# A hybrid attention and gated-MLP block on eight cores: the gating unit moved behind the attention, a part of the gate logits put in its place

## What is computed

```python
h = rmsnorm(x, norm1_g)                       # x: (4, 4096, 1024) float32
q, k, v, f_logit, u, sv, gates = split(h @ w_in)   # 512, 512, 512, 8, 512, 512, 2048 columns
logf = log_sigmoid(f_logit + b_f)
y_a = forgetting_attention(q, k, v, logf) @ w_a    # 8 heads of 64, causal, cumulated log gates added
v2 = layernorm(gelu(sv), ln_v_g, ln_v_b)           # per 128 positions: mixed by w_sgu, per group of 64
y_b = (gelu(u) * (mix(v2, w_sgu) + b_sgu)) @ w_b
g_a, g_b = split(gates)
x = x + (sigmoid(g_a) * y_a + sigmoid(g_b) * y_b) @ w_o
x = x + square(relu(rmsnorm(x, norm2_g) @ w_up)) @ w_down
return rmsnorm(x, normf_g)
```

## Time and profile before

| | us |
|---|---|
| median of 3 runs | 1326.27 |
| lowest and highest | 1326.08, 1328.8 |
| the profiled execution | 1336.07 |
| span of its slowest core (core 7) | 1334.5 |
| span of its fastest core (core 0) | 1314.7 |

### The profile page before, as it was taken

One profiled execution on the slowest core, in us unless ns is written; L12 is line 12 of the kernel. 1 busy time (PEld: TensorE's weight loads), 2 busy tenths in 40 slices (PEclk: granted clock), 3 DMA queues, 4 the chain that ended last, 5 costly groups with the idle time before them and its releaser, 6 DMA issues.

```text
span 1334.5 us, 22415 instructions; the slowest of 8 cores (1314.7 to 1334.5 us)
## 1 busy us (share of the span) xinstructions
PE 1172.6 (88%) x7624; PEld 577.1 (43%) x7624; DVE 585.0 (44%) x951; ACT 482.1 (36%) x634; POOL 305.0 (23%) x278
## 2 busy tenths in 40 slices
PE   4577887869899878887999997999999999999994
PEld 1234444435455444444444443444444444444441
DVE  2355473243224666664222233653433434334357
ACT  2212224547788655665222223421111121111153
POOL 0112130110001434331322220033333232332320
PEclk9787978989999878997999998999999999999998
DMA  7824033151122113101431216332130320303015
GB/s 141 206 77 151 29 121 93 49 105 40 45 53 49 27 34 63 26 21 41 71 64 25 48 16 166 106 53 45 19 64 1 64 52 13 64 0 64 1 64 189
DMA packets 30942, 85.42 MB, mean 64 GB/s; under 512 B 5088, under 2 KB 13376, under 8 KB 25248
## 3 DMA queue, kind: packets, MB, share of 16 engines
q0 software_dynamic: 5312, 31.18, 14.2%
q1 hardware_dynamic: 25232, 52.78, 13.4%
q10 hardware_dynamic: 288, 0.03, 0.0%
HBM read 99.88 MB, written 13.17 MB: 85 GB/s over the span
## 4 chain that ended last, share of the span: by engine, by line
PE 75%; DVE 8%; DMA 8%; issue 4%; ACT 3%; SPq 1%; DVEq 0%; POOL 0%; ACTq 0%; POOLq 0%
PE pss L362 75%; ACT PT L366 2%; DMA xres<-xown 1%; DVE VP L384 1%; DMA QpT<-QT 1%; DMA WK<-wproj 1%; DVE hown L380 1%; DVE zz L380 1%; DMA scrt<-kst 1%; DMA xbuf<-xown 1%; DMA WQ<-wproj 1%; DVE hprev L380 1%; DMA xbuf<-xprev 1%; DVE uT L380 1%; DMA QpT<-scrq 1%
## 5 line engine op out<-in xcount | busy, mean ns | idle before, releaser
L366 ACT ACTIVATE PT<-pss 128x1024 bf16<-128x1024 f32 (+1 forms) x288 | 271.3, 973 | 161.7 <-PE pss L362 160.8
L374 DVE TENSOR_TENSOR x1T<-pss,x1T 128x512 f32<-128x512 f32 x256 | 176.1, 691 | 247.6 <-PE pss L362 219.2
L362 PE MATMUL pss<-QpT,KpT 86*128 86x512 bf16 (+3 forms) x640 | 179.2, 368 | 59.4 <-ACT PT L366 41.5
L362 PE MATMUL pss<-aT,fdn 128*128 128x512 bf16 x1024 | 226.7, 379 | 0.6 <-DVE x1T L374 0.6
L362 PE MATMUL pss<-h2T,fup 128*128 128x512 bf16 x1024 | 226.2, 379 | 0.0
L366 ACT ACTIVATE rl<-pss 128x512 f32<-128x512 f32 x128 | 76.3, 597 | 333.3 <-PE pss L362 327.8
L374 POOL TENSOR_TENSOR aT<-rl 128x512 bf16<-128x512 f32 x128 | 133.5, 1044 | 264.4 <-ACT rl L366 248.9
L362 PEld LDWEIGHTS pss<-aT,fdn 128*128 128x128 bf16 x1024 | 100.1, 98 | 121.7 <-issue 1.4
L362 PEld LDWEIGHTS pss<-h2T,fup 128*128 128x128 bf16 x1024 | 100.2, 98 | 120.8
L362 PEld LDWEIGHTS pss<-VP,PT 128*128 128x128 bf16 x2176 | 106.5, 101 | 78.9 <-issue 37.3
L362 PE MATMUL pss<-VP,PT 128*128 128x65 bf16 x2176 | 119.6, 199 | 16.4 <-DVE VP L384 15.9
(11 more groups left out here) (117 smaller groups left out, 1064.1 us busy)
## 6 DMA issues: line engine op xcount, KB each, us to landing
xbuf<-xown SPq DMA_DIRECT2D x8, 1024.0 KB, 8.3
xbuf<-xprev SPq DMA_DIRECT2D x8, 1024.0 KB, 9.1
xres<-xown SPq DMA_DIRECT2D x32, 256.0 KB, 3.2
fup<-w_up POOLq DMA_DIRECT2D x8, 1024.0 KB, 9.5
fdn<-w_down POOLq DMA_DIRECT2D x8, 1024.0 KB, 10.8
out<-ostg SPq DMA_DIRECT2D x32, 256.0 KB, 2.1
Wb<-wmrg POOLq DMA_DIRECT2D x8, 768.0 KB, 8.4
scrt<-kst SPq DMA_DIRECT2D x32, 128.0 KB, 2.8
```

The lines of the kernel that those rows point to most:

```text
L362: S.op("pe", lambda e, a=(out, lhsT, rhs, start, stop): e.matmul(a[0], a[1], a[2], start=a[3], stop=a[4]), r, w)
L366: S.op("act", lambda e, a=(out, in_, func, scale): e.activation(out=a[0], in_=a[1], func=a[2], scale=a[3]), r, w)
L374: S.op(eng, lambda e, a=(out, in0, in1, op): e.tensor_tensor(a[0], a[1], a[2], a[3]), r, w)
```

## The change

- **The gating unit leaves chunk 3.** It runs behind the last head as a stage of its own, with all 8 PSUM banks as its ring. Its gelu is now one ACT function (`AF.Gelu`) that reads the PSUM bank; the hand-made chain with `xs`, `zz` and `gg` goes. The last product (`vln`) moves from POOL to DVE.
- **Gate logits go into chunk 3.** For the first three of eight column blocks (NLG = 3) the 24 pairs of dc, I and branch are computed as fill pieces (`lg_q`), copied by DVE to float tiles `lg`, and used in merging in place of 16 of the 24 matmuls of these 12 rounds. Their weights `Wg` lie where `hprev` was. WU and WSV are loaded behind the first column block's logits, not as soon as the x buffers are free.
- **Squares** are taken on ACT alone, in eight pieces of 512 columns, woven between other pieces; before, POOL took 10 of the 16 halves of 2048 columns.
- **x loads** are in quarters, and from position 1 on they are issued on the POOL queue, not on SP. Position 1 is issued before WK. The start computes V of both positions first, then K and Q.
- **`wsTb`** is loaded at the end of chunk 0, and the DVE memset on it stands there too.
- **Banks**: a head's sums always lie in bank 4; the fill ring has banks 5, 6 and 7; the transposes of `yst` take a ring bank.
- Ln and Exp behind `rms_q` and `f_q` are written one or two pieces later (`later`).

```diff
+        WU, WSV = [at(n, 4096, BF16, OFF_W + 8 * KB * i) for i, n in enumerate(("WU", "WSV"))]
+        lg = [at("lg%d" % i, 512, F32, OFF_X0 + 2 * KB * i if i < 20 else OFF_W + (16 + 2 * (i - 20)) * KB) for i in range(24)]
+        Wg = [at("Wg%d" % i, 16 * 128, BF16, OFF_HP + 4 * KB * i) for i in range(2)]
+        g32 = [at("g32%d" % i, 512, F32, OFF_VP + (16 + 2 * i) * KB) for i in range(4)]
+        vln = [at("vln%d" % i, 512, BF16, OFF_VP + (24 + i) * KB) for i in range(4)]
+        stmp = [at("stmp%d" % i, 512, F32, OFF_VP + (28 + 2 * i) * KB) for i in range(2)]
+        uT = at("uT", 4 * T, BF16, OFF_VP, False)
...
+        Wb = [at("Wb%d" % i, 24 * 128, BF16, OFF_HP + 6 * KB * i) for i in range(2)]
...
-        def xload(pos, r=()):
+        def xload(pos, eng="pool"):
             own, I = order[pos]
             src = xown_d if own else xprev_d
             i_ = pos % 2
-            for hf in range(2):
-                ld("sp", xbuf[i_][:, hf * 2048:(hf + 1) * 2048], src[I, :, hf * 2048:(hf + 1) * 2048], B("xb%d%d" % (i_, hf)), r)
+            for hf in range(4):
+                bf = B("xb%d%d" % (i_, hf))
+                S.dma(eng, lambda e, a=(xbuf[i_][:, hf * 1024:(hf + 1) * 1024], src[I, :, hf * 1024:(hf + 1) * 1024]): e.dma_start(out=a[0], in_=a[1]),
+                      [], [bf], bf if eng == "pool" else Buf("xs%d" % hf))
...
-        xload(0)
+        xload(0, "sp")
         ld("pool", onesb[:], cst_d[:, 256:384], B("onesb"))
         ld("pool", wf[:], wf_d[:, :], B("wf"))
-        ld("pool", WV[:], wproj_d[0], B("WV"), [B("xb01")])
+        ld("pool", WV[:], wproj_d[0], B("WV"), [B("xb03")])
+        xload(1)
         ld("pool", WK[:], wproj_d[1], B("WK"))
-        xload(1, [B("WK")])
-        ld("pool", WQ[:], wproj_d[2], B("WQ"), [B("xb11")])
-        ld("sp", trif[:], cst_d[:, 128:256], B("trif"))
+        ld("pool", WQ[:], wproj_d[2], B("WQ"))
+        ld("sp", bexp[0:32, :], bexp_d[:, 0:32], B("bexp"))
+        ld("sp", trif[:], cst_d[:, 128:256], B("trif"), [B("xb13")])
...
+        def sq_q(pos):
             i_ = pos % 2
-            for hf, eng in enumerate(engs):
-                src, dst = xbuf[i_][:, hf * 2048:(hf + 1) * 2048], sq[:, hf * 2048:(hf + 1) * 2048]
-                if eng == "act":
-                    act(dst, src, AF.Square, [B("xb%d%d" % (i_, hf))], [B("sq%d" % hf)])
-                else:
-                    tt(eng, dst, src, src, ALU.mult, [B("xb%d%d" % (i_, hf))], [B("sq%d" % hf)])
+
+            def mk(kc):
+                return (0.0, lambda: act(sq[:, kc * 512:(kc + 1) * 512], xbuf[i_][:, kc * 512:(kc + 1) * 512], AF.Square,
+                                         [B("xb%d%d" % (i_, kc // 2))], [B("sq%d" % kc)]))
+            return [mk(kc) for kc in range(8)]
...
+        def lg_q(dc, I, j):
+            li = (dc * 4 + I) * 2 + j
+            wg = Wg[dc % 2]
+
+            def mms(pb, kc):
+                mm(ps(pb), wg[:, j * 1024 + kc * 128:j * 1024 + (kc + 1) * 128], hown[:, kc * T + I * 512:kc * T + (I + 1) * 512], kc == 0, kc == 7,
+                   [B("Wg%d" % (dc % 2)), B("ho%d_%d" % (kc, I))], [PB[pb]])
+
+            def evict(pb):
+                cp("dve", lg[li][:], ps(pb), [PB[pb]], [B("lg%d" % li)])
+            return unit_q(mms, evict)
+
+        def gload(dc):
+            ld("pool", Wg[dc % 2][:], wmrg_d[dc][:, 1024:3072], B("Wg%d" % (dc % 2)))
...
+                gt, gB = g32[b % 4], B("g32%d" % (b % 4))
+                s6, s6B, b4 = st6[b % 2], B("st6%d" % (b % 2)), b % 4
+                act(gt[:], ps(pb), AF.Gelu, [PB[pb]], [gB])
+                S.op("dve", lambda e, a=(s6[:, 0:6], gt[:]): e.bn_stats(a[0], a[1]), [gB], [s6B])
+                S.op("dve", lambda e, a=(mv[b4][:, 0:2], s6[:, 0:6]): e.bn_aggr(a[0], a[1]), [s6B], [B("mv%d" % b4)])
+                ts("dve", tv[b4][:], mv[b4][:, 1:2], EPS, None, ALU.add, ALU.bypass, [B("mv%d" % b4)], [B("tv%d" % b4)])
+                tt("pool", rsv[b4][:], tv[b4][:], mhalf[:], ALU.pow, [B("tv%d" % b4), B("mhalf")], [B("rsv%d" % b4)])
 
                 def nrm():
-                    gt, gB, b4 = gg[b % 2], B("gg%d" % (b % 2)), b % 4
                     ts("dve", gt[:], gt[:], mv[b4][:, 0:1], rsv[b4][:, 0:1], ALU.subtract, ALU.mult, [gB, B("mv%d" % b4), B("rsv%d" % b4)], [gB])
-                    tt("pool", vln[b % 6][:], gt[:], lng[:], ALU.mult, [gB, B("lng")], [B("vln%d" % (b % 6))])
+                    tt("dve", vln[b4][:], gt[:], lng[:], ALU.mult, [gB, B("lng")], [B("vln%d" % b4)])
                     vdone.add(b)
-                late.append([4, fin])
-                late.append([6, nrm])
+                later(2, nrm)
...
+                act(uT[:, cc * T + I * 512:cc * T + (I + 1) * 512], ps(pb), AF.Gelu, [PB[pb]], [B("uT%d_%d" % (I, q_)) for q_ in range(4)])
...
+            ld("pool", wsTb[:], wsT_d[:, :], B("wsTb"))
+            memset("dve", wsTb[64:128, :].rearrange("p (g i) -> p g i", i=128)[:, :, 0:64], 0.0, [B("wsTb")], [B("wsTb")])
...
-        squares(0, ("act", "act"))
-        run(rms_q(0))
+        run(sq_q(0) + rms_q(0))
+        flush_late()
         run(stt_q(0))
-        xload(2, [B("WQ")])
-        run(f_q(0))
-        for blk in range(4):
-            run(v_q(0, blk))
-        squares(1, ("act", "act"))
-        for p in range(4):
-            run(kq_q(0, p, False))
+        xload(2)
+        run(v_q(0, 0) + v_q(0, 1) + sq_q(1) + v_q(0, 2) + v_q(0, 3) + f_q(0))
         run(rms_q(1))
+        flush_late()
         run(stt_q(1))
         xload(3)
-        run(f_q(1))
-        run(kq_q(1, 0, False))
-        run(fin_tot(0))
-        run(kq_q(1, 1, False))
-        run(fin_cum(0))
-        run(kq_q(1, 2, False))
-        for kind in range(3):
-            run(fin_tr(0, kind))
-        run(kq_q(1, 3, False))
-        run(v_q(1, 0))
+        run(v_q(1, 0) + f_q(1) + v_q(1, 1) + v_q(1, 2) + fin_tot(0) + v_q(1, 3))
+        run(kq_q(0, 0, False) + fin_cum(0) + kq_q(1, 0, False) + kq_q(0, 1, False) + fin_tr(0, 0) + kq_q(0, 2, False) + fin_tr(0, 1) + fin_tr(0, 2))
         run(kq_q(0, 0, True))
         headload(0)
-        squares(2, ("act", "pool"))
-        for blk in range(1, 4):
-            run(v_q(1, blk))
-        for p in range(1, 4):
-            run(kq_q(0, p, True))
+        run(kq_q(0, 3, False) + kq_q(1, 1, False) + kq_q(1, 2, False) + kq_q(1, 3, False))
         headload(1)
-        ring[:] = [6, 7]
-
-        memset("dve", wsTb[64:128, :].rearrange("p (g i) -> p g i", i=128)[:, :, 0:64], 0.0, [B("wsTb")], [B("wsTb")])
+        run(weave(kq_q(0, 1, True) + kq_q(0, 2, True) + kq_q(0, 3, True), sq_q(2), 2))
+        flush_late()
+        ring[:] = [5, 6, 7]
...
+            t1 = kq_q(e, 1, False) + kq_q(o, 1, True) + [("pair", (c, 1))]
             t2 = kq_q(o, 2, False) + kq_q(e, 2, False) + kq_q(o, 2, True)
             if c < 3:
-                qs += rms_q(o + 2) + ev(lambda: squares(e + 2, ("pool", "pool")))
+                qs += weave(t1, sq_q(o + 2), 2)
+                qs += rms_q(o + 2)
...
+        NLG = 3
+
+        def lg_list():
+            qs = []
+            for dc in range(NLG):
+                for I in range(4):
+                    for j in range(2):
+                        qs += lg_q(dc, I, j)
+                if dc + 2 < NLG:
+                    qs += ev(lambda dc=dc: gload(dc + 2))
+                if dc == 0:
+                    qs += ev(lambda: (ld("pool", WU[:], wproj_d[3], B("WU")), ld("pool", WSV[:], wproj_d[4], B("WSV"))))
...
-            yb = 4 + n % 2
+            yb = 4
...
+                        tb = fbank()
                         for qb in range(4):
-                            mm(pss[:, yb * 512 + qb * 128:yb * 512 + (qb + 1) * 128], yst[yi][:, qb * 128:(qb + 1) * 128], identb[:], True, True,
-                               [B("yst%d" % yi), B("identb")], [PB[yb]])
-                        cp("dve", yaT[:, p * T + I * 512:p * T + (I + 1) * 512], ps(yb), [PB[yb]], [B("ya%d_%d" % (p, I))])
+                            mm(pss[:, tb * 512 + qb * 128:tb * 512 + (qb + 1) * 128], yst[yi][:, qb * 128:(qb + 1) * 128], identb[:], True, True,
+                               [B("yst%d" % yi), B("identb")], [PB[tb]])
+                        cp("dve", yaT[:, p * T + I * 512:p * T + (I + 1) * 512], ps(tb), [PB[tb]], [B("ya%d_%d" % (p, I))])
...
-                    wload()
+                    gload(0)
+                    gload(1)
...
+        ring[:] = [0, 1, 2, 3, 5, 6, 7, 4]
+        rk[0] = 0
+        bundle(0)
+        bundle(1)
+        run(ev(bias2))
+        for b in range(16):
+            run(sv_q(b) + u_q(b))
+            if b >= 3 and b % 4 == 3:
+                run(mix_q(b - 3) + (mix_q(b - 2)))
+            elif b >= 4 and b % 4 == 0:
+                run(mix_q(b - 2))
+            elif b >= 4 and b % 4 == 1:
+                run(mix_q(b - 2))
+        run(mix_q(14) + mix_q(15))
...
+                st_ = dc < NLG
+                for kc in range(0 if st_ else 8):
...
+                for j in range(2):
```

(3 more changed lines are left out.)

190 lines of the change are left out of this document (74 added, 116 removed).

## The result

The changed kernel takes **1286.36 us** (median of 4 runs, 1284.68 to 1287.47), the kernel before 1327.53 us (1326.08 to 1329.22): ratio 0.969, interval 0.967 to 0.971. It is 41 us faster, where 62.5 were forecast; 1264 was the time named and 1238 to 1292 the range, so the result lies in its upper part. Times of kernels leave out executions in which one die ran clearly longer at a lower granted clock. The profiled execution took 1284.68 us, on its slowest core (core 0) 1283.2; the fastest core had 1270.4.

What follows compares the result with a forecast made beforehand. Chunk 3's attention was held by ACT's queue waiting for DVE's hand-made gelu. Gains of 27 (chunk 3, gating, merging), 14.5 (start), 7, 11, 2 (chunks 0 to 2) and 1 sum to 62.5 us: 1264 us, range 1238 to 1292.

Steps and rivals of the forecast that it cites:

- Rival (b): Chunk 3 stays ragged, ACT pacing its steps at clock 0.89: stage 165 us, kernel 1288 us; chance 15%.
- the shifts: Chunk 3: third ring bank 5 us off; Wg wait 3, WU and WSV loads 3, single y bank 1 on.
- The third bank: Chunk 3: a third ring bank takes away most short waits for VP copies, 5 us off.
- Rival (a): Gating stage runs at PE's pace, DVE's wait for POOL hidden: 20 us less, kernel 1244 us; chance 12%.
- (c): Gating stage runs at 1.2 GHz because PE pauses for DVE: 40 us more, kernel 1304 us; chance 7%.
- (d): Kernel slower than before, over 82 of 183 us PE work in chunk 3 and gating at 1.2 GHz; chance 3%.
- rival (e): New start and load order bring nothing, memory being at its limit: 1285 us; chance 6%.
- the waits for QpT: Chunk 1: PE's waits of 10.1 and 4.7 us go with the WU and WSV transfers, 14.8 us less.
- The 4 us for VP: Chunk 1: part of the 6.3 us of waits for VP goes, 4 us less.
- The `wsTb` term: Chunk 1: DVE's memset waits for the late wsTb load, holding yst and a K copy: 8 us lost, 4 to 12.
- Banks 3 us less, y bank 1 us more: Chunk 2: third ring bank gains 3 us, single bank for head sums costs 1, net 2 us less.
- so nothing new comes to bound it: Merging: DVE's 1.38 us and POOL's 1.26 us still fit a 1.73 us round; stage 127.5 us.

Runs made afterwards that it cites:

- the version with slots: Changed kernel with merging's first three short weight blocks in own tiles, loaded with block 3 at the gating stage's start, Wo's load late: 1269.65 us, ratio 0.957.

## Why the prediction was right, and where it was off

**Direction and cause: right.** Chunk 3 was ragged because ACT's queue stood behind DVE: the run without Tanh took 51 us off it (at most 17 of them the Tanhs' own time), and the changed chunk has clock 1.00 and 6.3 us of waits for Exps. Rival (b) fell.

**Chunk 3, 141 forecast, 135.6 measured.** The base, chunk 2's ratio of 1.14 times 122, gives 139; the shifts added 2. The Wg wait (3 us) and the contention of WU and WSV with head loads (3 us) didn't occur: no wait for either is in the list. The third bank was counted at 5 us for `VP` waits, which chunk 3 hardly has: no V is made there. The 5 us came off all the same, by another cause than forecast: the ratio came from chunk 2, which carries some 6 us of those waits, and the new chunk 3 has none. So 139 - 5 + 1 = 135 is what remains of the sum, and 135.6 was measured.

**Gating stage, 82 forecast, 75.7 measured.** The mechanism holds (DVE's 16 waits for `rsv`, confirmed by moving the normalisation). The size was high by a term taken from a stage in which POOL was loaded: statistics to the end of the power took 1.99 us (562.69 to 564.68) and not 2.29, with the power at 0.55 and not 0.84 us, and an sv unit without mixings went round in 3.35 us, not 3.9. Rival (a), the stage at PE's pace, is nearly what the edit made of it: 66.8 us, where 61 were counted. Rivals (c) and (d) fell: the granted clock was 0.92 in this stage and not near 0.5. PE did pause, 11.4 us in four places, and the clock is lowest where it did, in the last quarter of the stage:

```profile
540.00:560.00 20.00, 19.82 (x124) 8.97 (x123) 14.47 (x30) 6.24 (x11) 2.19 (x4) 1.00 0.00 1
...
580.00:598.80 18.80, 10.06 (x77) 4.82 (x75) 13.63 (x28) 6.68 (x10) 2.19 (x4) 0.84 0.01 2
```

The Trainium skill's case (TensorE: Matmul & The Clock Gate, "A second HAM failure mode: psum-queue depth-cycling"), by which (c) would have been likeliest, is not borne out by the trace: 0.84 is the lowest of its four quarters. The price of (d) was also added up wrongly: all 183 us at 1.2 GHz would have given 1264 + 183 - 20 = 1427 us, not 1365.

**Start and chunk 0: right**, within 1 us each, and rival (e) fell. In the start the course fits too: V of position 0 ended at 33 us (32 forecast), the scaling of position 1 began at 35. For chunk 0 the number fits, and the scalings are 0.75 us at most, where the earlier trace rows had 5.83 for two; but what those were worth to PE no run isolates, and the chunk's median moves by 2 us by itself.

**Chunk 1, 106 forecast, 106.8 measured: luck.** The forecast was 11 us less; the median fell by 2.1, from 108.9. The sum started from core 7, where the chunk took 117 us and the waits for QpT of the earlier trace rows came to 14.8 us. Core 6 had 14.2 us of them, the six others 7.0 to 9.2 us and a chunk of 108 to 110 us. So some 6 us of this term were a gain on two cores only. The 4 us for VP did not come either: PE still waits 6.1 us there. The `wsTb` term was 8 us (4 to 12), and its removal gave 12.1 us of the median, at the top of its range, as the clock's part was left out; the single bank for the sums, which the sum of this chunk left out, cost 3.0 us more. That these errors end at 106.8 is chance: the base was 8 us too high for the median, and the losses were put too low.

**Chunk 2, 105 forecast, 109.4 measured: wrong sign.** "Banks 3 us less, y bank 1 us more" failed on both halves. The `VP` waits came from a dependency on a name, not from a bank, and so stayed at 6.1 us; the single bank for the sums cost 2.4 us, not 1.

**Merging, 127.5 forecast, 148.5 measured: the step that failed.** It is the sentence "so nothing new comes to bound it", which looked at DVE and POOL only and put the weights' landing at nothing. The count of matmuls was right, as the version with slots shows. Missing was the question that the same text puts elsewhere: what is late next. Three blocks became three times as short, their weights kept one block of cover, and Wo's 2 x 1024 KB still stood between two of them. The earlier trace rows had the price: 11.2 us for 1024 KB, against 6.9 us of cover.

**Output projection, 1 forecast, 6.6 us less measured.** PE's wait at its end, of the kernel before and then of the changed one:

```profile
PE pss L362 <- ACT sq L366: 7.6, 3, 6.2
```
```profile
PE pss L359 <- ACT sq L363: 0.6, 1, 0.6
```

On the seven other cores of the kernel before this wait was 3.2 to 5.4 us, so its going is the larger part of the 6.6 us, not all of it. That more `xres` buffers are the reason was not tested.

**The base.** 62.5 us were summed against an execution of 1336.07 us and taken off a median of 1326.27. The profiled executions differ by 51.4 us, the medians by 41.2. The stages explain 11 us of the miss, and the other 10 are this: the profiled execution of the kernel before lay 8.5 us above its median (cores 6 and 7 took 1332.0 and 1334.5 us, the others 1325.0 at most), that of the changed kernel 1.7 us below. Terms that remove a wait of two cores count less in the median.

## What to carry to other kernels

Where an edit shortens a loop round, hold its new length against the time its next weights need from issue to landing, and look for a large transfer that is issued between them on the same queue; here room for one more block ahead brought 7 us (1276.8 to 1269.65) where fewer bytes brought nothing. Where an engine's queue stands before an operand, ask first whether that one operation can be made not to wait, before moving the whole unit. Where a matmul waits for a copy that it doesn't read, look at the names in its dependency list before giving it more buffers. And cost a wait by the cores that show it: a term read on the slowest core of one execution is a gain of the median only where the others have it too.
